# A two-layer diffusion trunk with a mixture of experts: how each layer ends, with three experts' rows kept on chip and the token rows asked for earlier

## The reference

```python
def _grouped_moe(h, w_router, b_router, w_gate, w_up, w_down):
    t = h.reshape(-1, shape[-1])
    aff = jax.nn.sigmoid((t @ w_router).astype(jnp.float32))
    ...            # the best of 4 groups, the 2 best of its 4 experts, gates normalised
    hid = jax.nn.silu(jnp.einsum('nd,edf->nef', t, w_gate)) * jnp.einsum('nd,edf->nef', t, w_up)
    out = jnp.einsum('nef,efd->nd', hid * gates[..., None].astype(hid.dtype), w_down)

x = x + g1 * o                                       # attention and output projection
x = x + g2 * _grouped_moe(_modulate(x, n2, sh2, sc2), ...)
...
y_prompt = _rms_norm(xc, final_norm_g)
y_sample = _rms_norm(xs, final_norm_g)
```

## Time and profile before

| | us |
|---|---|
| median of 3 runs | 1023.37 |
| lowest and highest | 1022.71, 1027.02 |
| the profiled execution | 1026.33 |
| its span | 1024.5 |

### The profile page before, as it was taken

One profiled execution on the slowest core, in us unless ns is written; L12 is line 12 of the kernel. 1 busy time (PEld: TensorE's weight loads), 2 busy tenths in 40 slices (PEclk: granted clock), 3 DMA queues, 4 the chain that ended last, 5 costly groups with the idle time before them and its releaser, 6 DMA issues.

```text
span 1024.5 us, 13521 instructions
## 1 busy us (share of the span) xinstructions
PE 940.8 (92%) x5209; PEld 460.4 (45%) x5209; DVE 348.8 (34%) x862; ACT 252.8 (25%) x604; POOL 131.8 (13%) x151
## 2 busy tenths in 40 slices
PE   4899989999999999987779998999999999988895
PEld 3345535555433444332354554565554344333342
DVE  2241167521752121111151005754157112121227
ACT  2220055421511111111151103554041111111124
POOL 4131000001111111110033100000121111110101
PEclk8999999999999999999989999999999999999999
DMA  9961376687999999999984026767927999999993
GB/s 345 395 233 36 145 275 247 247 351 305 376 371 391 395 392 393 399 413 413 384 298 151 20 83 225 296 243 289 423 87 278 389 385 389 397 407 413 415 397 155
DMA packets 58568, 313.64 MB, mean 306 GB/s; under 512 B 6826, under 2 KB 9094, under 8 KB 27520
## 3 DMA queue, kind: packets, MB, share of 16 engines
q1 hardware_dynamic: 50208, 288.54, 72.2%
q0 software_dynamic: 7424, 21.01, 5.9%
q10 hardware_dynamic: 864, 3.15, 0.8%
HBM read 300.01 MB, written 17.26 MB: 310 GB/s over the span
## 4 chain that ended last, share of the span: by engine, by line
PE 72%; DMA 19%; DVE 3%; SPq 2%; issue 2%; ACT 1%; POOL 1%; ACTq 0%; POOLq 0%; DVEq 0%
PE psum L1146 14%; DMA arena<-in_w_up 12%; PE psum L1571 8%; PE psum L1424 8%; PE psum L1212 7%; PE psum L1396 4%; PE psum L1387 4%; PE psum L1059 3%; PE psum L1542 3%; PE psum L1507 3%; DMA arena<-in_w_ada 3%; PE psum L1519 3%; PE psum L1158 2%; PE psum L1086 1%; DMA arena<-expert_rows 1%
## 5 line engine op out<-in xcount | busy, mean ns | idle before, releaser
L1146 PE MATMUL psum<-arena 128*64 128x512 f32 x480 | 217.3, 601 | 20.1 <-DMA arena<-in_w_up 20.0
L1149 PE MATMUL psum<-arena 128*64 128x512 f32 x480 | 217.7, 602 | 0.0
L1146 PEld LDWEIGHTS psum<-arena 128*64 128x64 f32 x480 | 64.6, 138 | 160.8 <-issue 157.8
L1212 PE MATMUL psum<-arena 128*64 128x512 f32 x480 | 110.9, 600 | 2.0 <-ACT arena L1741 0.9
L2210 DVE SCALAR_TENSOR_TENSOR arena<-arena,psum 64x512 f32<-64x512 f32 (+2 forms) x32 | 22.9, 714 | 247.8 <-ACT arena L1735 247.8
L1571 PE MATMUL psum<-arena 128*128 128x384 f32 x256 | 84.0, 488 | 0.6 <-PE psum L1571 0.6
L1424 PE MATMUL psum<-arena 128*128 128x384 f32 x256 | 83.4, 487 | 0.6 <-PE psum L1424 0.6
L1735 ACT ACTIVATE arena<-psum 64x512 f32<-64x512 f32 (+2 forms) x32 | 19.7, 617 | 254.3 <-PE psum L1149 233.0
L1149 PEld LDWEIGHTS psum<-arena 128*64 128x64 f32 x480 | 64.6, 138 | 0.0
L1424 PEld LDWEIGHTS psum<-arena 128*128 128x128 f32 x256 | 48.3, 190 | 34.6 <-issue 1.8
L1571 PEld LDWEIGHTS psum<-arena 128*128 128x128 f32 x256 | 48.2, 190 | 34.9 <-issue 2.5
(11 more groups left out here) (323 smaller groups left out, 1181.0 us busy)
## 6 DMA issues: line engine op xcount, KB each, us to landing
arena<-in_w_down SPq DMA_DIRECT2D x64, 1024.0 KB, 29.0
arena<-in_w_gate SPq DMA_DIRECT2D x64, 1024.0 KB, 27.4
arena<-in_w_up SPq DMA_DIRECT2D x64, 1024.0 KB, 27.7
arena<-in_w_ada SPq DMA_DIRECT2D x24, 2048.0 KB, 8.3
arena<-in_w_in SPq DMA_DIRECT2D x6, 2048.0 KB, 15.8
arena<-in_w_out SPq DMA_DIRECT2D x4, 2048.0 KB, 8.0
arena<-expert_rows SPq DMA_DIRECT2D x12, 512.0 KB, 10.9
arena<-in_w_in SPq DMA_DIRECT2D x2, 1664.0 KB, 14.1
```

The lines of the kernel that those rows point to most:

```text
L1146: ins = nc.tensor.matmul(bank[b][0:MAIN, :], hg[:, k, 0:MAIN], row(wg[half], k), start=(k == 0), stop=(k == KD - 1))
L1149: ins = nc.tensor.matmul(bank[b][MAIN:P, :], hg[:, k, 0:MAIN], row(wu[half], k), start=(k == 0), stop=(k == KD - 1))
L1212: ins = nc.tensor.matmul(bank[6][MAIN * j:MAIN * j + MAIN, :], hidT[:, c, 0:MAIN], down_row(w[half], c)[:, 512 * j:512 * j + 512], start=( ...
```

## The change

Both layers end in the same way. `SUMMED` is 3: the rows of the units 13 and 14 (`PAIR`, 64 each) stay in `y_sb[1]`, those of unit 15 in `y_least`, four blocks of 32 rows under one another. `last_sel` has 128 rows, and `least_sel` repeats unit 15's 32 rows four times, so that its product reads the quarter in which a feature block lies. Four experts are fixed; their order in the queue changes with it. SP asks for the token rows after unit 15's gate and up weights and before the down weights of units 14 and 15. The six pair products run right behind down(15), ahead of the branch. The turning of token rows is marked as a transpose. Layer 1 runs `combine`, turns `xT` back and does the final norm; the gain comes by a broadcast load. The spare units, where they are needed, run before `combine` in both layers and the token rows are then loaded again.

```diff
-FIXED = 3
+FIXED = 4
...
-SUMMED = 2
+SUMMED = 3
+PAIR = (E_ALL - 3, E_ALL - 2)
+SCATTERED = ((E_ALL - SUMMED + 1) // 2, (E_ALL - SUMMED) // 2)
...
-    order = gate_up(0) + gate_up(1) + down(0) + gate_up(2) + down(1)
-    order += down(2) + gate_up(3)
-    for u in range(4, AHEAD):
+    order = gate_up(0)
+    for u in range(1, AHEAD):
         order += gate_up(u) + down(u - 1)
...   SP
-                down_weights(l, 2, 2)
+                gate_up_weights(l, 3, 3)
                 sp.wait_ge(htok_ps, 2 * NT * (l + 1))
                 sp.wait_ge(ordered, l + 1)
...
                 sp.wait_ge(xt_ps, unit_of(l, 0) + 1)
-                before = ranked(FIXED)
-                gate_up_weights(l, FIXED, before)
-                for u in range(FIXED + 1, AHEAD):
+                down_weights(l, 2, 2)
+                before = FIXED - 1
+                for u in range(FIXED, AHEAD):
                     e = ranked(u)
                     gate_up_weights(l, u, e)
+                    if u == LEAST:
+                        for i in range(2):
+                            sp.wait_ge(y_out[i], 16 * SCATTERED[i] * (l + 1))
+                        sp.wait_ge(slot_free, max(loads.last(l, p) for p in END_PLACES) + 1)
+                        token_rows(y_hi_in, y_lo_in)
                     down_weights(l, u - 1, before)
                     before = e
...   TensorE
+            def least_product(k):
+                r = slice(TAIL * (k // 2), TAIL * (k // 2) + TAIL)
+                nc.tensor.matmul(bank[SUM_BANK[k]][:, 0:TOK], y_least[r, P * (k % 2):P * (k % 2) + P], least_sel[r, :], start=False, stop=False)
...
                 hidden_T(unit_of(l, units[-1]), frees=steady)
                 down(l, units[-1])
+                if units[-1] == LEAST:
+                    pair_products(l)
...   combine
+                pair_product(6)
+                for k in (0, 2, 4, 6, 1, 3, 5):
+                    least_product(k)
...
                     for t in range(NT):
                         ins = nc.tensor.matmul(bank[SUM_BANK[k]][:, P * t:P * t + P], y_hi[:, t, P * k:P * k + P], ident, start=False,
-                                               stop=t == NT - 1)
+                                               stop=t == NT - 1, is_transpose=True)
...
+                for half in range(2):
+                    for k in range(4 * half, 4 * half + 4):
+                        pe.wait_ge(scat_done, 8 * l + max(k + 1, 3 * half + 3))
+                        for t in range(NT):
+                            ins = nc.tensor.transpose(bank[END_BANK[t][half]][:, P * (k % 4):P * (k % 4) + P], xT[:, k, P * t:P * t + P], ident)
+                    ins.then_inc(turned_ps, 1)
...   ScalarE: the scales follow hidden_copy(15)
                 hidden_copy(unit_of(l, units[-1]))
+                if units[-1] == LEAST:
+                    scales(l, 0)
                 y_copy(unit_of(l, units[-1]))
...   VectorE: the mixes lie around the copy of unit 15
+                if units[-1] == LEAST:
+                    mix(l, 0, 0)
                 y_copy(unit_of(l, units[-1]))
+                if units[-1] == LEAST:
+                    mix(l, 0, 1)
...   VectorE, the final norm
+                for t in range(NT):
                     r = rsum[:, t:t + 1]
+                    dve.wait_ge(end_std, t + 1)
+                    st.did(v.reciprocal(r, r))
                     st.sync()
+                    for half in range(2):
+                        c = slice(512 * half, 512 * half + 512)
+                        ins = v.scalar_tensor_tensor(y_lo[:, t, c], bank[END_BANK[t][half]], r, gain_row[:, c], ALU.mult, ALU.mult)
+                    ins.then_inc(y_ready, 1)
```

More of the change, by code:

```diff
@@ L553, in overflow, with mixed_before @@
                     pass_over(eng, owned(1))
+                if again:
+                    again()
             with eng.Else():
[L555 to L569, removed]
+                pass_over(eng, [(s, at, share * sum(SPARE) // SPARE[0]) for s, at, share in owned(0)] + list(early))
+        def mixed_before(l, again):
+            return 2 * NT * (2 * l + again)
         @block.sync
@@ L676, in spare_loads @@
                     sp.wait_ge(y_spare[l], 16 * sum(SPARE[0:o + 1]))
-                if l == DEPTH - 1:
-                    break
+                if not more:
+                    sp.wait_ge(slot_free, loads.last(l, GAIN_ROW_PLACE) + 1)
+                    sp.dma_start(gain_row, a["final_norm_g"].partition_broadcast(P)).then_inc(gain_row_in, 16)
                 sp.wait_ge(routed, l + 1)
-                overflow(sp, lambda o: [], spare_loads)
-                for i in range(2):
-                    sp.wait_ge(y_out[i], 16 * (E_ALL - SUMMED) // 2 * (l + 1))
@@ L684, in _ @@
[L684 to L693, removed]
@@ L1132, in last_rows, with least_rows, gate_up @@
                 ins.then_inc(last_ps, 1)
-            def gate_up(l, u, frees=False, between=None):
+            def least_rows(l):
+                pe.wait_ge(last_hot_ready, 2 * l + 2)
+                pe.wait_ge(last_ready, 2 * l + 1)
+                for t in range(NT):
+                    ins = nc.tensor.transpose(bank[7][:, P * t:P * t + P], least_hot[:, t, :, :].rearrange("p j n -> p (j n)"), ident)
+                ins.then_inc(last_ps, 1)
+            def gate_up(l, u, frees=False):
                 q = unit_of(l, u)
@@ L1295, in experts @@
                 for i, u in enumerate(units):
-                    gate_up(l, u, frees=steady and i >= 2, between=x_early if ends and u == LAST[1] else None)
+                    gate_up(l, u, frees=steady and i >= 2)
                     if u == 0:
@@ L1635, in layer @@
                     keep_clock(1)
-                experts(l, list(range(AHEAD)), ends=l == DEPTH - 1)
+                experts(l, list(range(AHEAD)))
                 def owned(o):
@@ L2237, in experts @@
                         copy_slots(unit_of(l, units[i + 1]))
-                    if ends and u == LAST[0]:
-                        gate_diagonals()
                     if u == 0:
@@ new lines, in mix @@
+            def mix(l, again, half):
+                c = slice(512 * half, 512 * half + 512)
+                for t in range(NT):
+                    if half == 0 and not again:
+                        dve.wait_ge(y_lo_in[t], 16 * (l + 1))
+                    if half == 0 and again:
+                        dve.wait_ge(y_again, 32 * NT * (l + 1))
+                    dve.wait_ge(y_scaled, mixed_before(l, again) + NT * half + t + 1)
+                    v.scalar_tensor_tensor(y_hi[:, t, c], y_lo[:, t, c], w_tok[:, NT + t:NT + t + 1], y_hi[:, t, c], ALU.mult,
+                                           ALU.add).then_inc(y_mixed, 1)
@@ L2301, in end_norm, with mix_again @@
+            def mix_again(l):
+                for half in range(2):
+                    mix(l, 1, half)
+            def end_norm():
+                dve.wait_ge(end_squares, NT)
+                v.tensor_scalar(sums[:, 0:NT], stat[:, 0:NT], 1.0 / D, EPS, ALU.mult, ALU.add).then_inc(end_part, 1)
+                dve.wait_ge(gain_row_in, 16)
+                for t in range(NT):
                     r = rsum[:, t:t + 1]
-                    dve.wait_ge(end_std, NT * again + i + 1)
-                    st.did(v.reciprocal(r, stat[:, 3 + t:4 + t]))
+                    dve.wait_ge(end_std, t + 1)
+                    st.did(v.reciprocal(r, r))
```

384 lines of the change are left out of this document (126 added, 258 removed).

## The result

| | before | after |
|---|---|---|
| median, same chip (runs) | 1023.04 us (4) | 1033.51 us (4), 1030.64 to 1037.34 |
| ratio | | 1.009, 95% interval 1.0066 to 1.0115 |
| profiled execution, span | 1026.33, 1024.5 | 1030.64, 1028.7 |

A forecast was written before the change was run, and what follows sets the result against it. The prediction took each expert phase to end at the pace at which weights land, set by the slowest DMA engine. Layer terms of 2.5 and 5.7 sum to 8.2 us over the median 1023.37: 1031.6 us, range 1018 to 1041.

The forecast's parts named there:

- Last down weights 7.1 us later: End of each layer's weight queue: rows ahead (7.8 us), less one scatter (0.7), delay the last down half 7.1 us.
- Rival 2: Weight queue: the rows fit into DMA engines that ran dry, half the delay goes, 1024.5 us; chance 0.25.
- Wait of 5 to 6 us before down(14): TensorE near each layer's end: idle 5 to 6 us until the first of down(14)'s weights land.
- From the last landing to the first addition, 8.45 us: Layer end: down(15) 1.25, pair products 4.1, settling 0.5, seventh 0.7, least products 1.4, transposes 0.4, then 0.1 us.
- Rival 4: Layer ends: seven least products run serially (+3.4 us a layer), low clock costs 1 a layer, 1040.4 us; chance 0.12.
- the 2.4 us that the rule: TensorE's tiling-mode changes, four a layer: draining at each would cost both layers 2.4 us more, 1034.0 us.
- Layer 0, +2.5: Layer 0's ending, to VectorE's last added column: 530.8 against 528.3, 2.5 us later.
- FIXED 4, 3.4 us in layer 1 and 0 in layer 0: Expert 3's weights issued before the routing result: 3.4 us earlier in layer 1 (bounds 0 and 5.2), layer 0 nothing.
- The rival with a stream that comes ahead: Weight queue: the closed issue gap reaches the landings, dry engines take 2 us of rows, 1016.8 us; chance 0.18.
- Layer 1, +5.7: Layer 1's ending through the final norm's last product: 1025.0 against 1019.27, 5.7 us later.
- Clock, 0 taken: Down(14)'s second half and down(15) may run at 1.2 GHz, 0 to 1.8 us a layer; 0 taken, covered by loads.
- The mechanism forecast: Both layer ends: last down weights land 7 us later and products stand behind them, 1027 to 1036 us; chance 0.45.

The follow-up runs named there:

- experiments 2: Kernel after with y_hi's three row loads kept ahead of down(14)'s weights and y_lo's three moved behind down(15)'s: 1025.74 us, ratio 1.0016 to before.
- experiment 3: Kernel after with all token rows loaded behind down(15)'s weights and unit 15's copy ahead of scales and mixes: 1024.19 us, ratio 1.0002 to before.
- Experiment 5: Kernel before with FIXED 4, and layer 0's token rows turned as one-pass transposes: 1020.4 us, ratio 0.9967 to before.
- second profile of after: Profile from running the kernel after again, unchanged: 1035.84 us, ratio 1.011 to before.
- experiment 4: FIXED and its load order swapped alone: after with FIXED 3, 1038.89 us (1.0138); before with FIXED 4, 1019.67 us (0.9959).
- experiment 8: Unread TensorE fill products cut to the waits' length: in after 1033.53 us (1.01); in layer 0 of before with FIXED 4 1020.88 us (0.9972).
- experiment 1: Kernel after with all six token-row loads moved behind down(15)'s weights: 1028.17 us, ratio 1.0041 to before.
- experiment 7: Unread TensorE fill products during waits: in after 1042.08 us, in experiment 3's kernel 1023.68, in layer 0 of before with FIXED 4 1020.32.

## Why the time came out as forecast, and where the terms were off

- **Last down weights 7.1 us later.** 17.5 and 17.6 us behind the up half, where 17.5 was forecast. Rival 2, rows that fit into engines that had run dry, falls: experiments 2 and 3 move the landing in proportion to the bytes ahead. Of the two parts of the term, the 3 MB of rows took 7.6 us to land (7.8 taken); experiment 3, which has one scatter less than before and no rows ahead, lands 0.4 and 0.3 us earlier than before (0.7 taken).
- **Wait of 5 to 6 us before down(14).** 6.14 and 6.70.
- **From the last landing to the first addition, 8.45 us.** 8.1 in layer 0, 8.85 in layer 1, where the slow down(14) ended so late that down(15) stood behind it. The least products took 1.57 (1.4 taken), the additions 5.29 (5.5). Rival 4's serial products did not come. The chain shows no gap at the changes between full width, 32 rows and transposes: the transposes start at 521.11, when the 14 records before them end (519.61 + 1.57 = 521.18; the ends of products are modelled). So the 2.4 us that the rule in the Trainium skill, TensorEngine Tiling (Array Packing), Key Properties, would have added are not in this trace.
- **Layer 0, +2.5: measured +3.5.** This is the term that was too small. I ended the layer with VectorE's last addition. That came 30.9 us after the last up landing, before 29.0, so +1.9 of +2.5; but the projection stood 6.05 us behind it instead of 4.47. GpSimd adds the squares of each column pair in 0.99 us per instruction (L757) and had become the last in the chain: the norm's sums (L988) start 1.22 us behind VectorE's last addition, and all 24 of them stand there. Before, 18 of the 24 had run by then, and the last six started 0.6 us behind it. That is 1.3 of the 1.6 us; the rest is the spreading of the result (L1001), 0.81 us instead of 0.50. The Trainium skill, GPSIMD Engine Reference, section 3.1 on elementwise work, has GpSimd about twice as slow as VectorE for an addition of two operands. The trace comes near it: VectorE's product of two operands over the same 384 columns takes 548 ns (L1871), 1.8 times less. Experiment 5 fits: VectorE ended 0.5 us earlier and the norm did not. In the second profile of after the layer cost +5.8, 2.3 us of it by the slow clock.
- **FIXED 4, 3.4 us in layer 1 and 0 in layer 0.** 3.6 and 0.3 between the two milestones (before against after); by the whole kernel 3 to 5 us (experiment 4). The rival with a stream that comes ahead falls with the 0.3.
- **Layer 1, +5.7: measured +5.8**, with two errors that cancel. From the last addition to the end took 7.5 us (1017.84 to 1025.34) where I had 6.3, as ScalarE squares four half rows in 2.4 us before the first root. The landing came 1 us earlier than forecast, 0.7 of it because the last up half took 27.0 us from issue to landing instead of 27.7. So the layer's sum is right by luck to within 0.1.
- **Clock, 0 taken.** The row was read rightly and the level was 0.50. Against the tails of experiment 8 it costs 0.2 and 1.1 us in the first profile of after and 2.5 and 2.8 in the second, more than the 0 to 1.8 a layer that were allowed for. By the medians it is not told from zero.
- **What the forecast missed without being hurt:** it took the copy of unit 15 behind a mix to cost nothing. With the rows ahead of it that is so; experiment 1 shows 3.98 us when they are not. The old ending of layer 1 was worth something too: without the queue's part (experiment 3 against before with FIXED 4) the new one still makes tail 1 3.1 us longer. I didn't try which piece of it that is; together with 1.0 in tail 0 it makes up the 4.4 us by which experiment 3 is slower than before with FIXED 4. From the last down landing to the end the forecast's sum has 20.3 us where before took 18.3; it became 21.6. Before, its broadcast products and transposes ran in TensorE's wait for the last up half and down(14) took 3.65 us; in experiment 3 it took 5.31 in layer 1.

The mechanism forecast is the one that the runs show, rows ahead of the weights and a chain behind the weights. That the total came within 1 us is in part luck: profiled executions of after differ by 8.4 us, and the layers' terms were off by 1 us and by two errors of about 1 us that cancel.

What stays open: where the 3 to 5 us come from by which profiled executions differ ahead of the first expert phase, what makes executions of one kernel spread by 6 to 7 us, and how much of the 3.1 us is clock and how much the longer norm.

## What to carry to other kernels

When a queue is never empty, moving a load ahead doesn't make anything arrive sooner as a whole; it picks who is last. Put last the load with the shortest chain behind it: here 8 to 10 us from the last landing to the last addition hung on rows that came behind the weights, 13 to 14 on weights that came behind the rows. Before making a step quicker, look one engine further: GpSimd's additions, which the forecast left out, stood behind VectorE's and took what little VectorE had won.

## What the hardware showed

- 3 MB ahead in the queue cost the load behind them 7.2 to 7.6 us and half of it 3.7 to 4.6 (against experiment 3), although the mean DMA share was below one while the last loads were still under way. No view shows the 16 engines one by one, so that some of them had run ahead is an inference: in this window down halves of 1 MB land every 2.5 us, and 307 GB/s move only 0.77 MB in that time. The window 506 to 511 of after (the last three columns are granted clock, DMA share, GB/s):

```profile
506.00:511.00 5.00, 4.74 (x16) 1.57 (x16) 0.00 (x0) 0.00 (x0) 0.00 (x0) 0.68 0.76 307
```

- TensorE's granted clock after a wait for the same load differed from execution to execution of one kernel (down(14) 5.11 us after a wait of 6.14, 6.50 after 7.42). With the long fill ahead of it, it took 3.65 us in all five places (experiment 7).
- Seven products of two records each on alternating groups of 32 rows, 14 records of 384 columns, took 1.57 us, where 14 records at full width took 4.78. At a granted clock of 0.50 they took 2.94 (experiment 1).
